# Mixed and forgetting attention: the value product of a head pair stands behind the first scores of the next slot, its copy and low part one phase later

## What is computed

```python
# mixed attention: 8 windowed heads, 4 block heads, 4 heads that keep the top 128 keys
s = q @ k.T * 64**-0.5 + bias;  p = softmax(where(valid, s, -inf));  o = p @ v
_, idx = lax.top_k(score, 128)            # keys that a sparse head may see
x = x + concat([out_a, out_b, out_c]) @ w_out
# forgetting attention: 16 heads
logits = q @ k.T + (c[t] - c[s]);  p = softmax(causal(logits));  o = p @ v
h = h + rms_norm(concat(o) @ w_o, gain)
```

## Time and profile before

| | |
|---|---|
| Median of 3 runs | 3237.36 us (3237.35 to 3238.93) |
| The profiled execution, its own time | 3236.22 us |
| Its span, first to last instruction | 3234.5 us |
| Mean granted TensorE clock | 0.993 |
| Slots of `mix_0` / `mix_1` / `fox` | about 461 to 572 / 1409 to 1514 / 2686 to 2797 us of the span |

### The profile page before, as it was taken

How to read it: one execution, slowest core, us unless ns; L and a number is a source line. 1 busy time by engine, 2 the same in 40 slices (tenths; PEclk the granted TensorE clock), 3 DMA queues, 4 the chain that set the end, 5 groups by cost and what they waited for, 6 DMA issues and landing times.

```text
span 3234.5 us, 42440 instructions
## 1 busy us (share of the span) xinstructions
PE 3166.4 (98%) x14834; PEld 2543.0 (79%) x14834; DVE 1757.6 (54%) x2719; ACT 1159.1 (36%) x1878; POOL 536.4 (17%) x482
## 2 busy tenths in 40 slices
PE   8999999999999999999999999989999999999998
PEld 6788876788888888776888877668888886778887
DVE  4434577543445344585543454557656656586474
ACT  4323245322223222354322232634324335343242
POOL 0000346200020000264100030231000422310004
PEclk9999999999999999999999999999999999999998
DMA  4355331333333323321333323122333231223332
GB/s 125 97 138 147 101 100 34 90 97 93 97 98 98 104 85 104 80 66 43 95 103 90 102 77 115 46 59 72 107 88 101 65 100 42 59 72 103 92 96 80
DMA packets 540652, 288.02 MB, mean 89 GB/s; under 512 B 13603, under 2 KB 536582, under 8 KB 540544
## 3 DMA queue, kind: packets, MB, share of 16 engines
q1 hardware_dynamic: 535936, 273.32, 29.3%
q0 software_dynamic: 4608, 13.30, 1.4%
HBM read 284.30 MB, written 10.02 MB: 91 GB/s over the span
## 4 chain that ended last, share of the span: by engine, by line
PE 86%; DVE 6%; issue 3%; ACT 3%; POOL 2%; DVEq 0%; DMA 0%; ACTq 0%; POOLq 0%
PE bank L1852 69%; PE bank L1866 5%; PE bank L2093 2%; PE bank L1883 2%; PE bank L2135 2%; PE bank L1949 2%; PE bank L2158 1%; DVE norm_t L1341 1%; DVE w_lo L1251 1%; ACT w_hi L793 1%; POOL probs L687 1%; PE bank L2018 0%; ACT tap_v L939 0%; PE bank L1904 0%; DVE prod L1471 0%
## 5 line engine op out<-in xcount | busy, mean ns | idle before, releaser
L793 ACT ACTIVATE w_hi<-w_raw 128x1024 fp32r<-128x1024 f32 (+2 forms) x477 | 533.6, 1119 | 1427.2 <-PE bank L1852 787.4
L1852 PE MATMUL bank<-h_hi,w_hi 128*128 128x512 f32 x2548 | 999.8, 392 | 7.1 <-DVE h_lo L1281 3.7
L1852 PE MATMUL bank<-h_hi,w_lo 128*128 128x512 f32 x2548 | 991.9, 389 | 0.0
L1852 PE MATMUL bank<-h_lo,w_hi 128*128 128x512 f32 x2536 | 986.9, 389 | 0.0
L1251 DVE TENSOR_TENSOR w_lo<-w_raw,w_hi 128x1024 fp32r<-128x1024 f32 (+1 forms) x445 | 616.7, 1387 | 472.0 <-ACT w_hi L793 471.8
L1852 PEld LDWEIGHTS bank<-h_hi,w_hi 128*128 128x128 f32 x2548 | 477.5, 187 | 119.6 <-issue 14.2
L1852 PEld LDWEIGHTS bank<-h_hi,w_lo 128*128 128x128 f32 x2548 | 477.5, 187 | 101.2
L1852 PEld LDWEIGHTS bank<-h_lo,w_hi 128*128 128x128 f32 x2536 | 475.4, 187 | 99.8 <-issue 1.7
L1852 PE MATMUL bank<-act_hi,w_hi 128*128 128x512 f32 x924 | 360.6, 390 | 0.0
L1852 PE MATMUL bank<-act_lo,w_hi 128*128 128x512 f32 x924 | 360.4, 390 | 0.0
L1852 PE MATMUL bank<-act_hi,w_lo 128*128 128x512 f32 x924 | 360.3, 390 | 0.0
(11 more groups left out here) (323 smaller groups left out, 3973.7 us busy)
## 6 DMA issues: line engine op xcount, KB each, us to landing
w_raw<-in_ffn_w_gate_dram SPq DMA_DIRECT2D x88, 512.0 KB, 3.8
w_raw<-in_ffn_w_up_dram SPq DMA_DIRECT2D x88, 512.0 KB, 3.8
w_raw<-in_ffn_w_down_dram SPq DMA_DIRECT2D x64, 704.0 KB, 4.5
w_raw<-in_ffn_w_in_dram SPq DMA_DIRECT2D x88, 512.0 KB, 3.8
w_raw<-in_ffn_w_out_dram SPq DMA_DIRECT2D x32, 704.0 KB, 4.6
w_raw<-in_w_in_dram SPq DMA_DIRECT2D x34, 512.0 KB, 3.8
w_raw<-in_a_w_qkv_dram SPq DMA_DIRECT2D x24, 512.0 KB, 3.9
w_raw<-in_w_out_dram SPq DMA_DIRECT2D x16, 512.0 KB, 3.8
```

The costliest lines, as they stand in the source:

```text
L793: nc.scalar.activation(split_home(c)[0][:, 0:nk, 0:cols], raw[c % 2][:, 0:nk, 0:cols], ACT.Copy).then_inc(hi_ready, 1)
L1852: mm = nc.tensor.matmul(result(c)[0:cols, :], w[:, k, 0:cols], x[k], start=(k == 0 and n == 0), stop=(k == nk - 1 and n == 2))
```

## The change

Three edits in `pair_slots` of three engines, with nothing added or removed. On PE the value product of pair p-1, which stood at the end of slot p-1, stands in part 0 of slot p, between the first scores of pair p+1 and the first transposes of pair p; the product of the last pair stays where it was. On ACT `pair_out` of pair p-1 moves from the head of slot p to behind the first transposed copies and exponentials, ahead of the weight rounding `hi`. On DVE `pair_low` of pair p-1 moves from the head of slot p to behind `pair_max` of part 0, the weight's low part and the top-k rounds of part 0, ahead of `pair_max` of part 1.

```diff
--- before.py
+++ after.py
@@ -1025,13 +1025,13 @@
 
                 for p in range(-1, NP):
                     nxt = p + 1 < NP
-                    if p >= 1:
-                        pair_out(stage, p - 1)
                     for part in range(3):
                         if p >= 0:
                             pair_turned(stage, p, part)
                         if nxt:
                             pair_exps(stage, p + 1, part)
+                        if part == 0 and p >= 1:
+                            pair_out(stage, p - 1)
                         if part == 0 and p + 1 + lead(stage) <= NP + 1:
                             hi(q0 + p + 1 + lead(stage))
                         if part == 0 and p == NP - 1:
@@ -1593,8 +1593,6 @@
 
                 for p in range(-1, NP):
                     nxt = p + 1 < NP
-                    if p >= 1:
-                        pair_low(stage, p - 1)
                     if nxt:
                         pair_max(stage, p + 1, 0)
                     if p >= 0:
@@ -1604,6 +1602,8 @@
                     if p == NP - 1:
                         third_low(q0 + NP + 2)
                     rounds(p, 0)
+                    if p >= 1:
+                        pair_low(stage, p - 1)
                     if nxt:
                         pair_max(stage, p + 1, 1)
                         pair_sums(stage, p + 1, 0)
@@ -2177,6 +2177,8 @@
                             if part == 0:
                                 wait_evacuated(pe, q0 + p + 1)
                             pair_scores(stage, p + 1, part)
+                        if part == 0 and p >= 1:
+                            pair_values(stage, p - 1)
                         if p >= 0:
                             pair_turn(stage, p, part)
                         if p + lead(stage) < NP:
@@ -2186,8 +2188,7 @@
                             gemm_blocks(q0 + NP + s, blocks, *of_heads)
                     if p == 0:
                         pe.wait_ge(vt_ready, VT_FIRST[stage] + (KT if stage == "fox" else 4))
-                    if p >= 0:
-                        pair_values(stage, p)
+                pair_values(stage, NP - 1)
                 gemm_blocks(q0 + NP + 1, range(5, 7), *of_heads)
                 gemm_blocks(q0 + NP, range(7, KT), *of_heads)
                 gemm_blocks(q0 + NP + 1, range(7, KT), *of_heads)
```

## The result

The changed kernel takes 3256.65 us (median of 4 runs, 3255.22 to 3259.55), the kernel before 3237.36 in the same comparison: ratio 1.0065, 95% interval 1.0053 to 1.0077. It is slower, by 19.3 us. The forecast was 3253.6, so the sign and most of the size came, and 3.0 us were missed.

The account below looks back on a forecast made before the run. PE, busy 98% of the span, was taken to bound the kernel. Terms 6.5 + 6.2 + 0.7 + 2.0 + 0.8 = 16.2 us on the profiled 3236.22 gave 3252.4, with 1.1 for the median 3253.6; range 3247 to 3258.

Parts of the forecast that it names:

- The loop through the transposes: `fox` slots 1 to 6: ACT's copy and DVE's low part lengthen the chain between transposes, 1.09 each, 6.5 us.
- The unfinished division: `fox` slots 1 to 6: first scores wait for DVE's division into `proj`, 1.03 each, 6.2 us.
- B: Rival for `fox`: the division is not a wait, only the loop counts; 3247.4 us, 7%.
- C: Rival for `fox`: the loop absorbs both moved instructions, only the division counts; 3247.1 us, 7%.
- D: Rival: both `fox` terms hidden, mixed attentions pay alone; 3240.2 us, no measurable change, 3%.
- The forgetting attention as a whole: All of `fox`: loop 6.5, division 6.2 and last slot 0.7 us, 13.4 in all.
- Slot 4 of the mixed attentions: PE's wait for POOL's scaling grows as `w_hi` and POOL's `w_lo` move later: 0.4 taken twice, 0.8 us.
- All behind it, `pen` too, keeps its time: Mixed attentions, slot 5: DVE's moved low part fits its idle time with 0.24 left, so no cost.
- The last slot: Slot 7: late low part makes a 2.6 us PE hole; 1.0 us per mixed attention, 0.7 in `fox`.
- rival E: New PE holes in slot 7, perhaps `fox`, lower the clock: 2 to 6 us more, 3256 to 3260, 10%.
- Rival A: Mixed attentions, slot 5: `pen` comes earlier, its 3.45 us wait goes; 3244.7 or 3231.3 us, 3%.
- The sum: All terms over the whole kernel: 16.2 us more, 3253.6 us predicted, +0.50%.

Follow-up runs that it names:

- experiment 4: Kernel before, with only DVE's `pair_low` moved to its new place: 3242.67 us, ratio 1.0024.
- 3: Changed kernel with PE's value product back in its old place, ACT's `pair_out` and DVE's `pair_low` still moved: 3249.38 us, ratio 1.0042.
- 11: Changed kernel, with DVE dividing the next unit of `fox` ahead of the slot's last reciprocals: 3256.63 us, ratio 1.0066.
- 6: Changed kernel, with POOL's `w_lo` held back until DVE's scaling is over, in the mixed attentions' last slots: 3257.68 us, ratio 1.0067.
- 7: Kernel before, with POOL's `w_lo` in slot 5 of the mixed attentions held back to lie beside DVE's scaling: 3243.31 us, ratio 1.0025.
- experiment 9: Kernel before, with the change in the mixed attentions alone and slot 5's four remaining top rounds in its first part: 3231.06 us, ratio 0.9983.
- Experiment 5: Changed kernel, with ACT's and DVE's old order in the last slot of all three attentions: 3251.07 us, ratio 1.0045.
- experiment 2: Kernel before, with the change in the forgetting attention alone: 3250.82 us, ratio 1.0045.
- experiment 8: Kernel before, with the four remaining top rounds of slot 5 in its first part, in the mixed attentions: 3231.18 us, ratio 0.9982.
- experiment 1: Kernel before, with the change in the two mixed attentions alone: 3242.59 us, ratio 1.0019.
- experiment 10: As experiment 9, but with ACT's and DVE's old order in the mixed attentions' last slot: 3228.47 us, ratio 0.9977.

## Where the prediction was right, and which steps failed

- **The loop through the transposes, 6.5.** Right. Distance 9.27 for the 9.3 announced; its halves measured apart at 0.60 (experiment 4) and 0.49 (3 against 4), together 1.09 a slot.
- **The unfinished division, 6.2.** Right: waits of 0.96 to 1.01 at six slot starts for 1.03. Taking it away alone made the slots of `fox` 6.3 us shorter (3). What I wrote of it, that only DVE coming earlier could shrink it, was half right: with DVE in time 0.8 of the wait stays (11). Rivals B, C and D are out; the two terms neither hide nor feed each other.
- **The forgetting attention as a whole**: 13.6 us in the profile (from 4.8 behind before at slot 0 to 18.4 behind at its end) and 13.8 alone, for 13.4 predicted. Six slots of 2.12 make 12.7 of it, and the last slot 0.76, where I had 0.7.
- **Slot 4 of the mixed attentions, 0.4 each.** Right: the slot takes 0.45 and 0.40 more. The wait for POOL is 1.05 for 0.74, so 0.3 of it. The row of after:

```profile
518.18 0.55 PE L2135 MATMUL bank<-ident,probs 128*128 128x128 f32 x3 [1.05 <-POOL probs L687]
```

- **"All behind it, `pen` too, keeps its time".** This step failed: a term put at nothing, which measured 0.5 us at each `pen` wait. Its margin of 0.24 was reckoned on DVE's queue alone, and the sentence after it said that POOL's `w_lo` moves with `w_hi`, without asking what DVE does at that moment. `w_lo` moved from 535.27 to 536.22; before, 0.53 of it lay on the scaling, now 1.05 does, and DVE stands still for that time (6 and 7 show it from both sides).
- **The last slot, 1.0 for each mixed attention.** The hole was foreseen (2.42 for about 2.6), and the 1.0 is right for what it does by itself: 1.0 in `mix_0` of experiment 9, where the clock stayed at 1.00. The term was mis-sized because it left out the clock, which I kept apart as rival E at 10%: it measured 2.17 in `mix_0` and 2.14 in `mix_1`. In `mix_0` the fill behind the hole takes 1.45 us for 0.8 and the step from the last transposes to the value product 2.11 for 1.74, together 1.0 of the 2.17. Experiment 5, which removes the hole, gives 5.6 back, the clock with it.
- **Rival E's half in `fox`.** In the profile of the changed kernel the waits of 0.9 and 1.0 left the matmuls of `fox` at full speed. But of the five profiled kernels that have all of the change in slot 6 of `fox`, three (experiments 2, 5 and 11) show a clock of 0.66 to 0.72 there and 1.3 to 1.6 us more in that slot. So E came in both halves, the second in some runs only, and 10% was too little.
- **Rival A**, an earlier `pen`, did not come by the change, but the place it named is the one worth working on: the rounds, moved on purpose, gave 5.1 us (8).
- **The sum.** Slots 4 to 7 of the two mixed attentions, up to the fill behind the last value product, took 5.8 us more in the profile, where I had 2.8: 0.9 in slot 4, 0.5 in slot 5, 0.1 in slot 6 and 4.3 in slot 7. That is the miss of 3 us in size; experiment 1 gives 5.6 for them. Slot 5 alone does not add up so simply: it grew by 0.66 in `mix_0` and shrank by 0.20 in `mix_1`, though both `pen` waits grew by 0.5, for in `mix_1` of before the clock was low for longer behind that wait. And some luck is in the profiled total: 0.9 us came back between `mix_1` and `fox`, where the two programs do not differ, and 0.6 came on outside the span.

## What to carry to other kernels

An instruction that an engine off the path runs while it would wait anyway costs nothing; moved out of there, it costs its full length wherever it lands in a chain that PE already waits for. Before a product is moved behind the next scores, ask what it covered: here it hid a division whose input is the matmul just before, and no order of the other engines brings that back. When a third engine's long instruction shifts, look at what it now lies beside, and leave the old order where nothing follows, such as in a last slot.

## What the runs showed of the hardware

- A DVE `TENSOR_SCALAR` that meets a running POOL `TENSOR_TENSOR` stands until that has ended: 2573, 1325, 1204 and 814 ns, where 474 to 486 (512 wide) and 290 (256 wide) are usual (experiment 7, the changed kernel, `pen` in experiment 8, the kernel before); each ends 0.14 to 0.28 us behind POOL's instruction. `MAX8` (0.43), `MATCH_REPLACE8` (0.41) and the custom maxima (0.56 and 0.29) beside the same POOL instruction kept their times.
- The granted clock behind a hole was not the same each time. Behind one of 2.42 us in slot 7 of `mix_0` it was 0.57, and behind one of 2.43 in the same slot of experiment 9 it was 1.00; that is 1.1 us of difference (8.43 against 7.30). Behind the 1.37 us hole of that slot it was 1.00 before, and 0.50 a little later in experiment 10.
- In slot 6 of `fox`, with waits of about 0.9 us each, it was 1.00 in the changed kernel and 0.66 in experiment 2, which has the same order there.
- Stretches at half clock can come or not come where the programs are the same: from 150 to 156 us the clock was 0.50 in the kernel before and 1.00 in experiment 8, and experiment 8 reached the first transposes of `mix_0` 3.3 us earlier. That is more than the smallest edits tried here are worth.
